# Three query chunks from the un-normalised residual, gates chunk by chunk, all centrings of one norm on VectorE

## The chip, the cores and the metric

The kernel runs on one core of a Trainium2 chip. The metric is the device time of one execution in microseconds (us), the median of three. The core has TensorE (PE in the rows, its weight loads PEld), VectorE (DVE), ScalarE (ACT), GpSimd (POOL) and SyncE (SP, which here only issues transfers).

## What is computed

A two-layer backbone on 512 latent tokens and 256 context tokens, D_MODEL = 1024, all in float32. Layer 0 mixes by latent attention and retention, layer 1 by a bidirectional mLSTM; a SwiGLU feed-forward (FFN) and layer norms follow each mixer. The change lies at the seam of the two layers, where the last norm of layer 0 feeds the input projection of layer 1:

```python
x = _layer_norm(ALPHA * x + ml[5] * _swiglu(_modulate(x, ml[3], ml[4]), ffn_w_in[l], ffn_w_out[l]),
                ln_g[l, 1], ln_b[l, 1])

def _mlstm_project(h, w_in, conv_w, conv_b, gate_b):
    qk, v, og, g = jnp.split(h @ w_in, [o1, o2, o3], axis=-1)
    qk = jax.nn.silu(_centred_conv(qk, conv_w, conv_b))
    q, k = jnp.split(qk, 2, axis=-1)
    ...
    g = (g.reshape(b, s, 4, H_M) + gate_b).astype(jnp.float32).transpose(2, 0, 3, 1)
    fwd = (g[0], jax.nn.log_sigmoid(g[1]))
    bwd = (g[2], jax.nn.log_sigmoid(g[3]))
```

Here `h` is the normalised and modulated `x`; `x` carries on as the residual.

## The kernel before

Tokens lie along the free axis: a 128x768 tile is 128 features of all 768 tokens, and `xT` holds eight of them (k or m = 0 to 7), so a norm over features is a sum over partitions, made by TensorE with a matrix of ones. Every float32 weight is split in two parts: ScalarE rounds it into a high part, GpSimd subtracts to get the low part, and a product is three matmuls (high x high, high x low, low x high), each in pieces of 512 and 256 columns. Weights come through a ring of four slots that SyncE fills. A slot's next load is issued when its last reader is done. Each engine runs its own list of instructions in the order written, and they meet only in counting semaphores, so one waiting instruction holds up all that is written behind it on its engine.

**The order at the seam.** The FFN of layer 0 ends with eight down-projection tiles (m = 0 to 7). VectorE merges each into `xT` (L2584), adds it to the running sum (L2595) and the square that ScalarE makes (L1872) to the other (L2609). TensorE then makes, from the un-normalised residual, two "query" feature chunks (f = 0, 1) of the mLSTM's input projection: `zqhi` and `zqlo` are the residual times the gain, split in two (L2150 on ScalarE, L2650 on VectorE), and the chunk is 24 matmuls for each f, as pieces of 258 and 256 columns over k (L1458). The mean and the deviation are put in afterwards, by `late_query` on VectorE (L2663 to L2667). `LN_AFTER = 3` puts the two sums of the norm (`ln_sums(1)`, L1340) after k = 2. Chunks f = 0 to 3 take weights that are loaded and split ahead (`fx_split` on ScalarE, L1911, `fx_low` on GpSimd, L3194); for f = 0 and 1 they go into slots of the FFN's weights that fall free with down tile 5 and down tile 7.

**The norm.** `layer_norm(1)` centres the tiles (x - mean), VectorE six (L2621) and GpSimd two (L3162), and VectorE multiplies each by 1/deviation (L2631). ScalarE makes the modulated `hT1[k]` (L1711, L1716) and VectorE its low part `hlo1[k]` (L2386), which counts `input_lo`.

**The projection.** `m_chunk(f, k)` is three matmuls for f < 4 (latent tokens alone) and six for f >= 4. Chunks 2 and 3 run together over k, chunk 3 `LAG` = 2 steps behind, and each step takes one unit of the modulation rows of layer 1 (L988: 16 matmuls of 256 columns, weights straight from the ring). The gates' projection, eight times six matmuls with `wg`, follows as one block, and then f = 4 to 7, each 48 matmuls, whose weight `whi1` and `wlo1` are a ring load, a split on ScalarE (L1695) and a subtraction on GpSimd (L3168). Chunks 0 to 7 are then convolved on VectorE (`conv(f)`, L2955 to L2957), from `cpad`, which ScalarE fills (`conv_in`: L2181 for f = 0, 1, and L2188, L2190 from the bank of PSUM for the others), and ScalarE's Silu follows (L2197, L2199). VectorE's list goes: late queries, modulation rows, conv(0), conv(1), `g_` (L2970, waits for the gates' evacuation L2209 on ScalarE), `lf` (L2974, waits for ScalarE's logarithm L2214), scans, conv(2), scans, conv(3), conv(4) to conv(7). TensorE's token-major tiles (L1024 to L1026) reuse the banks of chunks 5 to 7, and the third and later wait for their evacuation.

`LAG` is also read at the head of the kernel, where input chunks 0 and 1 of layer 0 run together over k in the same manner.

Of the kernel before, what the change touches and what calls it, by code (L numbers as in the profile page):

```python
# [126 lines left out]
def build(nc, x, c, ctx, c_ctx, mod_w, mod_b, ln_g, ln_b, ffn_w_in, ffn_w_out, ab_w_in, mla_q_norm, mla_w_uq,  # L127
# [354 lines left out]
    N_FX, N_Q, MOD_PRE = 4, 2, 3  # L482
    FX_ORDER, LN_AFTER = (2, 3, 0, 1), 3
# [179 lines left out]
    LAG = 2  # L663
# [162 lines left out]
    SUB_DVE, LEAD = KD - 2, 3  # L826
# [124 lines left out]
    def _(pe):  # L951
# [499 lines left out]
        for k in range(KD):
# [3 lines left out]
            for f in range(N_Q):  # L1455
                for w, z, st, sp_ in ((0, zqhi, k == 0, False), (0, zqlo, False, False), (1, zqhi, False, k == KD - 1)):
                    for a, b, at in Q_MM:
                        mm = pe.matmul(q_bank(f)[:, at:at + b - a], fx_chunk(f, w, k), z[:, k, a:b], start=st, stop=sp_)  # L1458
# [3 lines left out]

        rows2, rows3 = PS[2][:, T:], PS[3][:, T:]
        pe.wait_ge(ln_mean, 2)
        pe.wait_ge(ln_var, 2)
# [4 lines left out]
        mod_rows_stacked(1, 2, rows2, MOD_PRE, KD - 1)  # L1470
# [196 lines left out]
    def _(act):  # L1667
# [300 lines left out]
        def gate_loads():  # L1968

            act.dma_start(wgr[:, :, :], m_w_in[0].rearrange("(k p) n -> p k n", p=P)[:, :, C_MG:C_MG + 4 * H_M]).then_inc(gate_in, 16)  # L1970
            for g in range(4):
                act.dma_start(gb[32 * g:32 * g + H_M, :], m_gate_b[0, g].unsqueeze(1)).then_inc(gate_in, 16)

        def ffn(l):
# [75 lines left out]
            for at, (kind, i) in enumerate(seq):  # L2050
# [87 lines left out]
                else:  # L2138
# [1253 lines left out]
```

## Time and profile before

| | |
|---|---|
| median of 3 runs | 1805.11 us (1803.15 to 1807.51) |
| the profiled execution | 1806.19 us, its span 1804.5 us |
| PE busy | 1709.8 us (95 % of the span) |
| DVE, ACT, POOL busy | 998.3, 746.3, 855.4 us (55, 41, 47 %) |
| mean granted clock of TensorE | 0.985 of 2.4 GHz |

The rows below are of this one execution. Its own time is 1.69 us above its span and 1.08 us above the median. TensorE has work for 95 % of the span, so a time is gained or lost where TensorE stands idle, runs at the lower clock, or gets another amount of work. A row of a timeline has the start, the duration, engine and line, the operation, output and inputs with their shape, and, in brackets, how long the engine had stood idle before it and what released it.

### The profile page before, as it was taken

The page shows a single profiled execution, that of the slowest core. Times are in us where ns is not written, and L with a number is a line of the kernel's source. Part 1 is how long each engine was busy: PE and PEld are TensorE (multiplying, and loading weights), DVE is VectorE, ACT ScalarE, POOL GpSimd, SP SyncE. Part 2 cuts the span into 40 slices and gives each one's busy share as a digit, 9 for nine tenths or more (in the row PEclk, how much of TensorE's full clock was granted, in tenths as well). Part 3 has the DMA queues.
Part 4 walks back from the last instruction along what each step waited for, and adds up shares of the span by engine and source line. Part 5 has one row for each costly group of instructions (what it writes and reads, how often), then busy time and mean ns, then how long its engine had stood idle before and what let it go on. Part 6 is the DMA issues. An engine that isn't in the chain of part 4 may idle for free. (4 is left out here: it accounts for less than half of the span.)

```text
span 1804.5 us, 25317 instructions
## 1 busy us (share of the span) xinstructions
PE 1709.8 (95%) x10068; PEld 1436.5 (80%) x10068; DVE 998.3 (55%) x1622; ACT 746.3 (41%) x1151; POOL 855.4 (47%) x491
## 2 busy tenths in 40 slices
PE   4999999999899999999999997999978999999997
PEld 2888767755487889999999995877767879889886
DVE  2133345666567866464646679850287885333354
ACT  1531323655434853232323346452435583333344
POOL 1342212166536366464544651342335757566475
PEclk8999999999999999999999999999989999999999
DMA  9312242265412121212122243322201323333231
GB/s 349 89 47 59 59 140 94 94 185 172 135 47 71 47 70 59 82 56 84 49 78 63 71 132 127 101 59 70 59 1 47 94 70 118 94 94 115 72 117 59
DMA packets 189515, 163.81 MB, mean 91 GB/s; under 512 B 17742, under 2 KB 168494, under 8 KB 189398
## 3 DMA queue, kind: packets, MB, share of 16 engines
q1 hardware_dynamic: 187616, 160.92, 29.3%
q8 instruction: 80, 1.31, 0.3%
q10 hardware_dynamic: 1782, 1.28, 0.2%
q14 instruction: 37, 0.30, 0.1%
HBM read 160.08 MB, written 2.10 MB: 90 GB/s over the span
## 5 line engine op out<-in xcount | busy, mean ns | idle before, releaser
L3214 POOL TENSOR_TENSOR wsplit<-wsplit_raw,wsplit 128x512 fp32r<-128x512 f32 x108 | 149.8, 1407 | 118.4 <-DVE wsplit_raw L2753 105.6
L2584 DVE SCALAR_TENSOR_TENSOR xT<-ps,modc,xT 128x512 f32<-128x512 f32 (+1 forms) x168 | 104.1, 657 | 150.0 <-PE ps L1036 128.0
L1036 PE MATMUL ps<-us_a,wsplit 128*128 128x512 f32 x864 | 179.9, 355 | 3.1 <-DVE us_a L2854 1.7
L3199 POOL TENSOR_TENSOR wsplit<-ring,wsplit 128x1024 fp32r<-128x1024 f32 (+1 forms) x48 | 112.3, 2353 | 112.3 <-ACT wsplit L1918 112.3
L1036 PEld LDWEIGHTS ps<-us_a,wsplit 128*128 128x128 f32 x864 | 142.2, 188 | 27.8 <-DVE us_a L2854 2.4
L1036 PE MATMUL ps<-h,wsplit 128*128 128x512 f32 x720 | 156.0, 377 | 1.0 <-DVE hu L2677 1.0
L1930 ACT ACTIVATE wsplit<-wsplit_raw 128x512 fp32r<-128x512 f32 x108 | 68.4, 633 | 204.0 <-DVE wsplit_raw L2753 204.0
L1036 PE MATMUL ps<-us_b,wsplit 128*128 128x512 f32 x720 | 151.1, 354 | 1.7 <-DVE us_b L2854 1.7
L1036 PEld LDWEIGHTS ps<-h,wsplit 128*128 128x128 f32 x720 | 127.8, 188 | 26.1 <-DVE hu L2677 1.2
L3214 POOL TENSOR_TENSOR wsplit<-ring,wsplit 128x512 fp32r<-128x512 f32 x81 | 115.4, 1436 | 61.0 <-ACT wsplit L1930 61.0
L1036 PEld LDWEIGHTS ps<-us_b,wsplit 128*128 128x128 f32 x720 | 118.4, 188 | 21.5 <-DVE us_b L2854 2.1
L3168 POOL TENSOR_TENSOR wsp_in<-ring,wsp_in 128x1024 fp32r<-128x1024 f32 x22 | 53.1, 2413 | 163.1 <-ACT wsp_in L1695 163.1
L3289 POOL TENSOR_SCALAR lnbuf<-lnbuf,den 128x768 f32<-128x768 f32 (+1 forms) x48 | 84.9, 1775 | 88.5 <-DVE den L2542 87.9
L1026 PE MATMUL ps<-h,wsplit 128*128 128x384 f32 (+1 forms) x396 | 126.8, 320 | 0.0
L1025 PE MATMUL ps<-h,wsplit 128*128 128x384 f32 (+1 forms) x396 | 126.8, 320 | 0.0
L1024 PE MATMUL ps<-h,wsplit 128*128 128x384 f32 (+1 forms) x396 | 126.7, 320 | 0.0
L1036 PE MATMUL ps<-hx,wsp_in 128*128 128x512 f32 (+3 forms) x666 | 123.2, 346 | 2.5 <-DVE hx L2386 2.0
L3179 POOL TENSOR_TENSOR wsplit<-ring,wsplit 128x1024 fp32r<-128x1024 f32 x34 | 91.8, 2706 | 61.7 <-ACT wsplit L1938 61.7
L1036 PEld LDWEIGHTS ps<-hx,wsp_in 128*128 128x128 f32 (+1 forms) x666 | 102.8, 188 | 22.7 <-issue 3.7
L1024 PE MATMUL ps<-ts,wsplit 128*128 128x384 f32 (+1 forms) x360 | 112.9, 314 | 0.0
L1025 PE MATMUL ps<-ts,wsplit 128*128 128x384 f32 (+1 forms) x360 | 112.9, 314 | 0.0
L1026 PE MATMUL ps<-ts,wsplit 128*128 128x384 f32 (+1 forms) x360 | 112.9, 314 | 0.0
(495 smaller groups left out, 3959.8 us busy)
## 6 DMA issues: line engine op xcount, KB each, us to landing
ring<-in_ffn_w_in SPq DMA_DIRECT2D x88, 512.0 KB, 3.8
ring<-in_mod_w SPq DMA_DIRECT2D x77, 512.0 KB, 4.5
ring<-in_ffn_w_out SPq DMA_DIRECT2D x40, 512.0 KB, 3.4
ring<-in_m_w_in SPq DMA_DIRECT2D x24, 512.0 KB, 3.7
ring<-in_ab_w_in SPq DMA_DIRECT2D x21, 512.0 KB, 3.9
mod_rest<-in_mod_w SPq DMA_DIRECT2D x10, 512.0 KB, 15.8
ring<-in_ab_w_out SPq DMA_DIRECT2D x8, 512.0 KB, 4.3
ring<-in_m_w_out SPq DMA_DIRECT2D x8, 512.0 KB, 4.0
```

The costliest lines, as they stand in the source:

```text
L1024: pe.matmul(dst, s_hi, m_hi, start=first, stop=False)
L1025: pe.matmul(dst, s_hi, m_lo, start=False, stop=False)
L1026: return pe.matmul(dst, s_lo, m_hi, start=False, stop=last)
L1036: mm = pe.matmul(dst[:, a:b], w, h[:, a:b], start=st, stop=sp_)
L1930: act.activation(w_op(l, p, o, 0), src, ACT.Copy).then_inc(s_hi, 1)
L2584: ins = dve.scalar_tensor_tensor(xT[:, m, a:b], pair[:, a:b], modc[:, l, g, m, v:v + 1], xT[:, m, a:b], ALU.mult, ALU.add)
L3168: pool.tensor_tensor(w_lo[:, i % 2, :], ring[:, n % RING, :], w_hi[:, i % 2, :].bitcast(F32), ALU.subtract).then_inc(lo_made, 1)
L3179: pool.tensor_tensor(w_unit(place, 1), ring_unit(n), w_unit(place, 0).bitcast(F32), ALU.subtract).then_inc(lo_made, 1)
L3199: pool.tensor_tensor(down_unit(l, g, q, 1), down_ring(l, g, q), down_unit(l, g, q, 0).bitcast(F32), ALU.subtract).then_inc(lo_made, 1)
L3214: pool.tensor_tensor(w_op(l, p, o, 1), src, w_op(l, p, o, 0).bitcast(F32), ALU.subtract).then_inc(s_lo, 1)
L3289: pool.tensor_scalar(probs(i)[:, a:T], probs(i)[:, a:T], den[:, 1, i:i + 1], None, ALU.mult).then_inc(att_p, 1)
```

## The change

It touches eight things around the seam.

1. `N_Q` 2 to 3: query chunk 2 is made from the un-normalised residual too, after the sums of the norm (`q_part(2, k)`, 48 matmuls of 258 and 256 columns in place of 24 of 512), and takes a third `late_query`. The banks are dealt anew.
2. `LN_AFTER` 3 to 6: the sums of the norm come after k = 5.
3. VectorE makes all eight centrings of norm 1 (`SUBS`), GpSimd none.
4. The gates' projection runs chunk by chunk as `hlo1[k]` comes, with `m_chunk(3)` three steps behind (`LAG` 3, in the head too) and one unit of modulation rows behind each `m_chunk(3)`.
5. `late_query(0)` goes into VectorE's loop of the norm (at k = 2), and the low parts follow one step behind, not two.
6. The gates' weights are split before the norm, and their zeroing goes from GpSimd (one memset) to ScalarE (four of 128x512).
7. `fx_split` and `fx_low` for f = 0, 1 stand at m = 2 and 4, before at m = 3 and 5. On SyncE the loads of `mod_pre` stand behind the four loads of the fx weights, before ahead of them.
8. TensorE's waits ahead of f = 4 to 7 are placed anew.

```diff
-    N_FX, N_Q, MOD_PRE = 4, 2, 3
-    FX_ORDER, LN_AFTER = (2, 3, 0, 1), 3
+    N_FX, N_Q, MOD_PRE = 4, 3, 3
+    FX_ORDER, LN_AFTER = (2, 3, 0, 1), 6
...
-        return PS[(0, 1, 2, 3, 0, 2, 3, 0)[f]]
+        return PS[(0, 1, 2, 0, 2, 1, 3, 0)[f]]
...
-    LAG = 2
+    LAG = 3
...
-    SUB_DVE, LEAD = KD - 2, 3
+    SUBS, LEAD = (KD - 2, KD, KD - 2), 3
...
-        mod_rows_stacked(1, 2, rows2, MOD_PRE, KD - 1)
+        mod_rows_stacked(1, 2, rows2, MOD_PRE, KD - 3)
+        pe.wait_ge(ln_mean, 2)
+        for k in range(KD):
+            mm = q_part(2, k)
+            if k < 3:
+                mod_rows_stacked(1, 2, rows2, KD - 3 + k, KD - 2 + k)
+        mm.then_inc(ffn_tile, 1)
...
-        rest = [(1, 2, rows2, KD - 1)] + [(1, 3, rows3, k) for k in range(KD)]
+        pe.wait_ge(gate_lo, 1)
+        pe.wait_ge(ln_var, 2)
         for k in range(KD + LAG):
             if k < KD:
                 pe.wait_ge(input_lo, 2 * KD + k + 1)
-            for f, kf in ((2, k), (3, k - LAG)):
...
-            if k < len(rest):
-                l, g, rows, n = rest[k]
-                mod_rows_stacked(l, g, rows, n, n + 1)
-        pe.wait_ge(gate_lo, 1)
-        pe.wait_ge(late_q, 2)
-        for k in range(KD):
-            mm = project(PS[1], wg[:, 0, k, :], wg[:, 1, k, :], hT1[:, k, :], hlo1[:, k, :], k == 0, k == KD - 1, ALL_SEGS)
-        mm.then_inc(gate_mm, 1)
+                mm = project(PS[3], wg[:, 0, k, :], wg[:, 1, k, :], hT1[:, k, :], hlo1[:, k, :], k == 0, k == KD - 1, ALL_SEGS)
+                if k == KD - 1:
+                    mm.then_inc(gate_mm, 1)
+            if k >= LAG:
+                if k == LAG:
+                    pe.wait_ge(late_q, 1)
+                mm = m_chunk(3, k - LAG)
+                mod_rows_stacked(1, 3, rows3, k - LAG, k - LAG + 1)
+        mm.then_inc(ffn_tile, 1)
         mod_columns(1, 2, rows2)
         for f in range(4, 8):
+            if f == 4:
+                pe.wait_ge(late_q, 3)
...
             if f == 6:
+                pe.wait_ge(gate_ev, 4)
+            if f == 7:
                 pe.wait_ge(mod_ev, MOD_AT[1, 3])
-            if f >= 5:
-                pe.wait_ge(f_ev, f - 2)
+                pe.wait_ge(f_ev, 4)
...
-                        if l == 0 and m in (3, 5):
+                        if l == 0 and m in (2, 4):
                             fx_split(2 + m // 4)
...
-                layer_norm(1, lambda k: low_chunk(2, k, hT1, hlo1, hlo1_raw))
                 dve.wait_ge(gate_hi, 1)
...
-                for f in range(N_Q):
-                    late_query(f)
-                mod_rows_stacked(1, 2, PS[2][:, T:])
+                layer_norm(1, lambda k: low_chunk(2, k, hT1, hlo1, hlo1_raw), between=lambda k: late_query(0) if k == 2 else None, lag=1)
+                late_query(1)
+                late_query(2)
+                mod_rows_stacked(1, 2, PS[1][:, T:])
...
-                        pool.memset(wg[:, :, :, :].bitcast(F32), 0.0).then_inc(gate_zero, 1)
...
-            if l == 0:
-                pool.wait_ge(zq_lo, KD)
-                layer_norm(1)
```

**TensorE in the loop of the projection.** Before, in its last steps and at the start of the gates' block (`ps3<-hT1,fx1_hi` is chunk 3, `ps3<-ring,scol` a modulation unit; a unit's first matmul waits for its slot):

```order
L1036 MATMUL ps3<-hT1,fx1_lo 128x512
L988 MATMUL ps3<-ring,scol 2x256 [waits landed1]
L988 MATMUL ps3<-ring,scol 2x256 x3
...
L1036 MATMUL ps3<-hT1,fx1_hi 128x512
L1036 MATMUL ps3<-hlo1,fx1_hi 128x512
L1036 MATMUL ps3<-hT1,fx1_lo 128x512
L1036 MATMUL ps1<-hT1,wg 128x512 [waits late_q,gate_lo]
L1036 MATMUL ps1<-hT1,wg 128x256
```

After, in one step of the loop and at its end:

```order
L1040 MATMUL ps3<-hT1,wg 128x512 [waits input_lo]
L1040 MATMUL ps3<-hT1,wg 128x256
L1040 MATMUL ps3<-hlo1,wg 128x512
...
L1040 MATMUL ps3<-hT1,wg 128x256
L1040 MATMUL ps0<-hT1,fx1_hi 128x512
L1040 MATMUL ps0<-hlo1,fx1_hi 128x512
L1040 MATMUL ps0<-hT1,fx1_lo 128x512
L992 MATMUL ps0<-ring,scol 2x256 [waits landed3]
L992 MATMUL ps0<-ring,scol 2x256 x3
...
L992 MATMUL ps0<-ring,scol 2x256 [waits landed2]
L992 MATMUL ps0<-ring,scol 2x256 x3
L1002 MATMUL ps1<-kc,mrow 128x2 [waits mod_row]
L1002 MATMUL ps1<-kc,mrow 128x2 x7
L1040 MATMUL ps2<-hT1,whi1 128x512 [waits lo_made,late_q]
```

The gates' matmuls stand in the loop, a modulation unit comes only behind each chunk-3 step, so that three units follow the last gate matmuls, and the first matmul of chunk 4 (`whi1`) stands right behind the loop with the columns of modulation rows between.

**TensorE in the head**, where chunks 0 (`ps0`) and 1 (`ps1`) of layer 0's input run together. Before:

```order
L1036 MATMUL ps0<-hx,wsp_in0 128x512 [waits input_lo,lo_made]
...
L1036 MATMUL ps0<-hx,wsp_in0 128x256
L1036 MATMUL ps1<-hx,wsp_in0 128x512 [waits input_lo,lo_made]
L1036 MATMUL ps1<-hx,wsp_in0 128x256
```

After, from the same place:

```order
L1040 MATMUL ps0<-hx,wsp_in0 128x512 [waits input_lo,lo_made]
...
L1040 MATMUL ps0<-hx,wsp_in0 128x256
L1040 MATMUL ps0<-hx,wsp_in0 128x512 [waits input_lo,lo_made]
...
L1040 MATMUL ps0<-hx,wsp_in0 128x256
L1040 MATMUL ps1<-hx,wsp_in0 128x512 [waits input_lo,lo_made]
L1040 MATMUL ps1<-hx,wsp_in0 128x256
```

One more step of chunk 0 stands ahead of the first of chunk 1, and one more of chunk 1 is left for the end.

**ScalarE during the last down tiles** (`sg<-xT` the square of a tile, `zqhi` the gain times it, `wsplit<-ring` the split of a query weight). Before:

```order
L1872 ACTIVATE sg<-xT 128x768 [waits ln_sum2,z_ev]
L2150 ACTIVATE zqhi<-xT,gain 128x512
L1872 ACTIVATE sg<-xT 128x768 [waits ln_sum2,z_ev]
L2150 ACTIVATE zqhi<-xT,gain 128x512
L1911 ACTIVATE wsplit<-ring 128x2x512 [waits ffn_tile,landed0]
...
L1872 ACTIVATE sg<-xT 128x768 [waits ln_sum2,z_ev]
L2150 ACTIVATE zqhi<-xT,gain 128x512
L1911 ACTIVATE wsplit<-ring 128x2x512 [waits ffn_tile,landed1]
L1872 ACTIVATE sg<-xT 128x768 [waits ln_sum2,z_ev]
```

After:

```order
L1881 ACTIVATE sg<-xT 128x768 [waits ln_sum2,z_ev]
L2171 ACTIVATE zqhi<-xT,gain 128x512
L1920 ACTIVATE wsplit<-ring 128x2x512 [waits ffn_tile,landed0]
L1881 ACTIVATE sg<-xT 128x768 [waits ln_sum2,z_ev]
L2171 ACTIVATE zqhi<-xT,gain 128x512
L1881 ACTIVATE sg<-xT 128x768 [waits ln_sum2,z_ev]
...
L2171 ACTIVATE zqhi<-xT,gain 128x512
L1920 ACTIVATE wsplit<-ring 128x2x512 [waits ffn_tile,landed1]
L1881 ACTIVATE sg<-xT 128x768 [waits ln_sum2,z_ev]
```

The split that waits for down tile 5 stood ahead of the square of tile 3 and stands ahead of that of tile 2; the other, which waits for tile 7, moved from tile 5 to tile 4.

## Rows read from the trace of the kernel before

**Rows 1.** TensorE's waits, 1040 to 1200 us: waiter, releaser, total us, times, longest

```profile
PE ps L1458 <- POOL wsplit L3194: 3.8, 1, 3.8
PE ps L1024 <- ACT cpad L2190: 2.2, 1, 2.2
PE ps L1340 <- DVE lnbuf L2595: 2.0, 1, 2.0
PE ps L1036 <- DVE hlo L2386: 1.9, 1, 1.9
PE ps L1036 <- issue: 0.9, 1, 0.9
```

**Rows 2.** Stretches: start:end length, busy of PE, PEld, DVE, ACT, POOL, granted clock

```profile
1090.20:1096.30 6.10, 6.06 (x36) 5.87 (x36) 6.00 (x9) 1.46 (x2) 0.00 (x0) 0.72 0.28 86
...
1177.50:1184.00 6.50, 4.17 (x17) 2.77 (x16) 6.43 (x5) 4.51 (x9) 5.51 (x5) 1.00 0.29 82
```

**Rows 3.** ScalarE's timeline from 1141 us: start, duration, operation, idle before

```profile
1141.58 0.89 ACT L2209 ACTIVATE li<-ps,again 8x768 f32<-8x768 f32 x1 [4.93 <-PE ps L1036]
...
1144.33 0.90 ACT L2209 ACTIVATE gt<-ps,again 8x768 f32<-8x768 f32 x1
...
1182.31 0.60 ACT L2188 ACTIVATE cpad<-ps 128x512 f32<-128x512 f32 x1 [1.05 <-DVE cacc L2957]
```

**Rows 4.** VectorE's timeline, the gates' chain and one convolution that nothing held

```profile
1139.75 2.80 DVE L2957 SCALAR_TENSOR_TENSOR cacc<-cpad,vcol,cacc 128x512 f32<-128x512 f32 x1
1145.26 1.75 DVE L2970 SCALAR_TENSOR_TENSOR gbc<-gt 8x1536 f32<-8x1536 f32 x1 [2.71 <-ACT gt L2209]
...
1151.45 1.75 DVE L2974 SCALAR_TENSOR_TENSOR lf<-gt,lf 8x1536 f32<-8x1536 f32 x1 [2.55 <-ACT lf L2214]
...
1171.16 0.75 DVE L2957 SCALAR_TENSOR_TENSOR cacc<-cpad,vcol,cacc 128x512 f32<-128x512 f32 x1
```

**Rows 5.** VectorE's timeline in the norm, and of a late query

```profile
1108.19 0.95 DVE L2631 TENSOR_TENSOR xT<-xT,lnbuf 128x768 f32<-128x768 f32 x1
1109.06 0.94 DVE L2621 TENSOR_TENSOR xT<-xT,lnbuf 128x768 f32<-128x768 f32 x1
...
1127.38 0.16 DVE L2663 COPY again<-ps 128x2 f32<-128x2 f32 x1
...
1129.09 0.15 DVE L2663 COPY again<-ps 128x2 f32<-128x2 f32 x1
```

**Rows 6.** TensorE's timeline in the projection's loop and at its end

```profile
1123.72 0.61 PE L988 MATMUL ps<-ring,scol 128*2 128x256 f32 x8
...
1125.86 0.61 PE L988 MATMUL ps<-ring,scol 128*2 128x256 f32 x8
...
1132.89 0.52 PE L1036 MATMUL ps<-hT,wg 128*128 128x512 f32 x2
...
1141.41 0.65 PE L998 MATMUL ps<-kc,mrow 2*128 2x2 f32 x8
1141.99 0.62 PE L1036 MATMUL ps<-hT,whi 128*128 128x512 f32 x2
```

**Rows 7.** SyncE's next issue into the ring

```profile
1126.53 0.38 SPq L834 DMA_DIRECT2D ring<-in_m_w_in  x1
```

**Rows 8.** Transfers from 1124 to 1142 us: count, size, median us to landing

```profile
ring<-in_m_w_in SPq DMA_DIRECT2D x5, 512.0 KB, 4.3
```

**Rows 9.** GpSimd's timeline from 1135 us

```profile
1135.16 2.57 POOL L3168 TENSOR_TENSOR wlo<-ring,whi 128x1024 fp32r<-128x1024 f32 x1 [1.78 <-ACT whi L1695]
1137.73 1.44 POOL L3154 TENSOR_SCALAR xT<-xT,again 128x512 f32<-128x512 f32 x1
1139.14 2.85 POOL L3168 TENSOR_TENSOR wlo<-ring,whi 128x1024 fp32r<-128x1024 f32 x1
```

**Rows 10.** The head: GpSimd's subtraction and TensorE's wait for it

```profile
61.63 2.38 POOL L3168 TENSOR_TENSOR wsp_in<-ring,wsp_in 128x1024 fp32r<-128x1024 f32 x1 [16.44 <-ACT wsp_in L1695]
...
64.07 0.50 PE L1036 MATMUL ps<-hx,wsp_in 128*128 128x512 f32 x1 [0.57 <-POOL wsp_in L3168]
```

More of the change, by code:

```diff
@@ L921, in _ @@
             unit(n, view(n % RING, KD), w_in[:, :, f * P:(f + 1) * P])
+        sp.wait_ge(prod, BASE[1][0]["prod"])
+        for k in range(MOD_PRE):
+            sp.dma_start(mod_pre[:, k, :], mod_w[1, k * P:(k + 1) * P, 2 * D:3 * D]).then_inc(mod_pre_in, 16)
         mod_units(1, 2, MOD_PRE)
@@ L1447, in _, with q_part @@
         ffn(0)
+        def q_part(f, k):
+            for w, z, st, sp_ in ((0, zqhi, k == 0, False), (0, zqlo, False, False), (1, zqhi, False, k == KD - 1)):
+                for a, b, at in Q_MM:
+                    mm = pe.matmul(q_bank(f)[:, at:at + b - a], fx_chunk(f, w, k), z[:, k, a:b], start=st, stop=sp_)
+            return mm
         pe.wait_ge(zq_cols, 1)
@@ L1454, in _ @@
             pe.wait_ge(zq_lo, k + 1)
[L1455 to L1458 removed]
+            for f in range(2):
+                mm = q_part(f, k)
                 if k == KD - 1:
                     mm.then_inc(ffn_tile, 1)
[L1463 to L1465 removed]
+        rows2, rows3 = PS[1][:, T:], PS[0][:, T:]
         pe.wait_ge(mod_pre_in, 16 * MOD_PRE)
@@ L1972, in gate_loads, with gate_weights @@
                 act.dma_start(gb[32 * g:32 * g + H_M, :], m_gate_b[0, g].unsqueeze(1)).then_inc(gate_in, 16)
+            for part in range(2):
+                for k in (0, KH):
+                    ins = act.activation(wg[:, part, k:k + KH, :], kc[:, 0:KH * P].rearrange("p (k n) -> p k n", k=KH), ACT.Copy, scale=0.0)
+            ins.then_inc(gate_zero, 1)
+        def gate_weights():
+            act.wait_ge(gate_in, 16 * 5)
+            act.wait_ge(gate_zero, 1)
+            for g in range(4):
+                ins = act.activation(wg[:, 0, :, 32 * g:32 * g + H_M], wgr[:, :, H_M * g:H_M * (g + 1)], ACT.Copy)
+            ins.then_inc(gate_hi, 1)
         def ffn(l):
@@ L2158, in ffn @@
             if l == 0:
+                gate_weights()
                 layer_norm(1)
@@ L2168, in _ @@
         from_norm(1, hT1, hlo1_raw)
-        act.wait_ge(gate_in, 16 * 5)
-        act.wait_ge(gate_zero, 1)
-        for g in range(4):
-            ins = act.activation(wg[:, 0, :, 32 * g:32 * g + H_M], wgr[:, :, H_M * g:H_M * (g + 1)], ACT.Copy)
-        ins.then_inc(gate_hi, 1)
         def conv_in(f):
@@ L2200, in conv_out @@
                 act.activation(mk[:, f - 4, LAT:T], cacc[:, f % 2, LAT + 2:T + 2], ACT.Silu, bias=bias).then_inc(silu_ev, 1)
-        for f in range(N_Q):
+        for f in range(2):
             conv_in(f)
@@ L2609, in square_sum, with layer_norm @@
                 dve.tensor_tensor(s2_[:, 0:nt], s2_[:, 0:nt], sq_[:, m % 2, 0:nt], ALU.add).then_inc(ln_sum2, 1)
-        def layer_norm(i, split, between=None):
+        def layer_norm(i, split, between=None, lag=2):
             nt = NT[i // 2]
@@ L3160, in layer_norm @@
             pool.wait_ge(ln_mean, i + 1)
-            for k in range(SUB_DVE, KD):
+            for k in range(SUBS[i], KD):
                 pool.tensor_tensor(xT[:, k, 0:nt], xT[:, k, 0:nt], lnm[:, 0:nt], ALU.subtract).then_inc(ln_subp, 1)
```

67 lines of the change are left out of this document (32 added, 35 removed).

## The prediction

> **What bounds the kernel now.** I read the profile in this order: the table of TensorE's waits around the seam, to see how much idle time there is to win; then, backwards from the last of those waits, the timelines of ScalarE, VectorE and TensorE, to see which chain sets its end. From 1040 to 1200 us TensorE waits five times for 0.9 to 3.8 us [rows 1], and after the first it runs a while at half clock (0.72 of full over 1090.2 to 1096.3, [rows 2]). At first sight these 10.8 us are what the change is after. But the second largest, 2.2 us for ScalarE's `cpad` L2190, ends last: token tiles start again at 1183.2 only when chunk 7 has left its bank. That evacuation starts at 1182.3, released by VectorE's convolution L2957 [rows 3], and VectorE is busy for 6.43 of the 6.50 us around it, TensorE for 4.17 [rows 2]. So **VectorE's list, not TensorE's work, decides when TensorE goes on at 1183.2.** Whatever TensorE saves ahead of that only lengthens this wait, and it could come 2.2 us later at no cost. Followed back, VectorE's list stood idle last at 1151.4, for ScalarE's `lf`, and before that at 1145.3, for the last evacuation of the gates, L2209 [rows 4]. Those four evacuations start at 1141.6, with the end of the gates' block of matmuls [rows 3]. The chain is: gates done, 4 x 0.92 us on ScalarE, `g_` at 1145.26, logarithm, `lf` at 1151.45, then scans and convolutions to 1182.2. The question is when `g_` starts in the changed kernel.
>
> **The parts.**
>
> *Query chunk 2, `LN_AFTER`, the moved splits.* 48 matmuls of 258 and 256 columns stand in for 24 of 512: the same columns, a few per cent more. The wait of 3.8 us for the weights of the query chunks is gated by down tile 7, ScalarE's split and GpSimd's low part, all of which stay; the split moved to m = 2 makes ScalarE wait there for tile 5, so the squares come no earlier, and I leave 1090.2 where it is. The sums behind k = 5 take away the 2.0 us wait, and the loop to k = 7 ends some 3 us earlier. It moves the norm itself by +0.8 us (from 1102.2 to about 1103.0, since three more steps of 1.43 us stand ahead of the sums). All this is ahead of the wait at 1183.2 and counts only through the norm.
>
> *The norm.* VectorE makes two centrings more, 0.87 us each by the pitch of rows 5, and one late query in the loop, 1.71 us (the distance of the two copies in [rows 5]). The two centrings of GpSimd beside VectorE's first three are gone, so that the deviation, not the centrings, comes last, which pays for the later start: tile 0 is multiplied at about 1107.9 (before 1108.19). Then by the new list five operations to the first low part, 1107.9 + 5 x 0.87 = 1112.3; three more to each next, 1114.9; with the late query 1119.2; 1121.9.
>
> *The loop of the gates.* A step was 2.14 us (two chunks and a unit, from 1123.72 to 1125.86 [rows 6]). A gate piece is 1.06 us (eight from 1132.89 to 1141.41 [rows 6]), a chunk piece 0.70 (three matmuls of 0.23). The new step is 2.14 - 0.70 + 1.06 = 2.50 us. TensorE waits about 0.9 and 1.5 us for low parts 2 and 3 and is ahead of VectorE no more from step 3, at 1121.9. The last gate piece ends at 1121.9 + 4 x 2.5 + 1.06 = 1133.0, 8.4 us sooner than before. If ScalarE could evacuate at once, `g_` would follow at 1136.7. It can't: in ScalarE's list the splits of chunk 4's and chunk 5's weights stand ahead of the gates' evacuation, and these now come late.
>
> *The ring.* The weights of chunk 4 take the slot of modulation unit 4 of the second group. Before, this unit ended at 1126.47 [rows 6] and the load was issued at 1126.53 [rows 7]. Now a unit comes only behind each chunk-3 step: unit 0 in step 3, unit 4 in step 7, which ends at 1121.9 + 5 x 2.5 - 0.2 = 1134.2, and units 5 to 7 at 1.43 us each. So the load for chunk 4 goes out at **1134.2 instead of 1126.5, 7.7 us later**. It lands 4.3 us (median [rows 8]) to 4.9 us later, at 1138.5 to 1139.1; that for chunk 5, issued at 1135.7, lands at about 1140.0 to 1140.6. ScalarE (about 1 us a split, 0.7 a `cpad`) splits the first to 1140.0, fills `cpad` of chunk 1, splits the second to about 1141.3, and only then evacuates the gates: 4 x 0.92 = 3.7, to 1145.0 against 1145.23 before [rows 3]. **The 8.4 us that the gates gain are given back whole to this order of ScalarE's list.**
>
> *Convolution 1.* It needs that `cpad`, ready at 1140.7, and stands ahead of `g_`. GpSimd's subtraction for chunk 4 starts at 1140.1, and for chunk 5 at about 1143.4, 2.57 and 2.85 us long with 1.44 between [rows 9]. Before, the last step of this convolution took 2.80 us from 1139.75 and ended with GpSimd's subtraction, begun at 1139.14 [rows 4, 9], where an undisturbed one takes 0.75 [rows 4]: each of the two waits out the other. The Trainium skill ("SBUF — State Buffer", Who interferes with whom) says that an operation of VectorE with two inputs in SBUF and one of GpSimd that reads it shut each other out for the whole instruction; the trace agrees at this convolution. By that rule taking the centrings from GpSimd pays in the norm, and costs nothing here. I let its three steps alternate with GpSimd's: it starts at 1142.5, and ends at about 1147.4. Bounds: unhindered it would end by 1142.7 and the evacuation decides (`g_` at 1145.0, that is -0.25 us); held for one more GpSimd operation it ends at 1149. I take 1147.4 as nearest to the two holds of rows 4 and 9. `g_` moves from 1145.26 to 1147.45, **+2.2 us**.
>
> *Behind it.* Chunk 4 needs its low part, 1142.4: TensorE, through with loop and columns at 1139.2, waits 3.3 us, a new wait, and goes on at 1142.5 against 1141.99. If a stretch at half clock follows, as after the wait of 3.8 us (a loss of 6.1 x 0.28 = 1.7 us [rows 2]), it reaches the token tiles 2.2 us later than before, less the 0.9 us wait that goes: still ahead of VectorE's end at 1182.2 + 2.2. So the wait at 1183.2 moves by VectorE's +2.2.
>
> *The head.* Chunk 0 ends one step sooner: TensorE was continuous, a step is 1.05 us, but it waits 0.3 us for a low part on the way, so 0.7 to 0.8 us sooner. ScalarE's split and GpSimd's subtraction (from 61.63) come forward, and the wait of 0.57 us [rows 10] goes; 0.3 us of it is paid for by the new wait. **-0.3 us**; between 0 and -0.57.
>
> *Hidden at nothing:* the zeroing on ScalarE (it waits for tiles there), the memset off GpSimd, the order of SyncE's loads, the new banks, the third late query (VectorE waits for `cpad` 1 anyway).
>
> **Sum.** +2.2 - 0.3 = +1.9 us. The profiled execution, 1806.19 us, would be 1808.1; the median of before is 1.08 lower, and 1805.11 + 1.9 gives **1807.0 us**.
>
> **The rivals.** (a) *The evacuation decides, not convolution 1.* It falls between GpSimd's operations: -0.25 - 0.3, **1804.5**. For it: the convolution's start and GpSimd's are within 0.7 us, and the order is open. (b) *Fewer collisions behind `g_`.* VectorE and GpSimd meet again some four times before 1182; a shift can undo one or two, each worth 2.80 - 0.75 = 2.05 us. With conv(1) free as well VectorE would be 0.25 + 4.1 earlier; but TensorE, 0.5 later at chunk 4 and 0.9 earlier by the wait that goes, then sets the end, at 2.2 + 0.4 = 2.6 us sooner: 1805.1 - 0.3 - 2.6 = **1802.2**. Against it: the three engines shift by about the same 2 us, so that the pattern stays. (c) *The other side: a longer hold of VectorE's chain.* One more collision, +2.05, or the weights of chunk 5 land a microsecond late because TensorE's short waits at steps 2 and 3 bring the half clock (1.7 us [rows 2], which delays unit 4 and all behind it by as much): 1807.0 + 1.7 to 2.05 = 1808.7 to 1809.1, with both **1810.8**, with one about 1809. It decides once `g_` starts after 1149.2. (d) *The waits that the change takes from TensorE reach the end* (2.0, 1.9 and 0.9 us [rows 1]): 1805.1 - 4.8 = **1800.3**. This holds only if the wait at 1183.2 isn't the chain that I read it as, and if chunk 4's weights come before the loop ends.
>
> **Chances.** Forecast 0.45, (a) 0.2, (b) 0.06, (c) 0.22, (d) 0.07. A measurement of this kernel can tell 0.2 %, 3.6 us, from no change: faster is under 1801.5, slower above 1808.7. (d) and a little of (b) are faster, 0.09; (c) is slower, and 0.06 of the forecast's case by its upper bound for convolution 1 (1149), together 0.28; the rest, 0.63, lies between. The range, 1802.0 to 1810.5, leaves out (d) and the upper part of (c), about half of it.
>
> **What would show it.** After, in the profile: TensorE's wait before chunk 4 (`whi`), 3 us, released by GpSimd's subtraction (L3168 before); the first `in_m_w_in` load issued near 1134; ScalarE's gate evacuations ending at 1145.0 with idle ahead of the splits for the transfer; VectorE's `g_` near 1147.4 with no idle before it; the token tiles' wait ended near 1185.4. The prediction is wrong if `g_` starts before 1144, if the wait for `cpad` is gone, or if TensorE's clock falls in the loop of the gates.

## The result: slower, by more than the range allowed

Both kernels were run ten times.

| | before | after |
|---|---|---|
| median of 10 runs | 1806.29 us (1803.15 to 1815.83) | 1815.35 us (1812.25 to 1820.33) |
| the profiled execution, its span | 1806.19, 1804.5 us | 1812.25, 1810.3 us |
| PE busy | 1709.8 us | 1714.0 us |
| mean granted clock of TensorE | 0.985 | 0.985 |

The ratio is 1.0040, 95 % interval 1.0026 to 1.0055: the changed kernel is 4.7 to 9.9 us slower. The forecast was 1.9 us slower, with a range that ended at 1810.5.

**How the two traces are laid over each other.** The two profiled executions differ by 1.4 us before the seam, in the transfers at the start, so from here on times at the seam are counted from the first query matmul (1090.22 us in the trace before, 1088.79 after). The middle column has what the forecast gives on the same count:

| us from the first query matmul | before | forecast | after |
|---|---|---|---|
| the last query matmul ends | 19.1 | | 26.4 |
| first low part `hlo1[0]` starts | 23.2 | 22.1 | 27.4 |
| gates' last matmul ends | 51.3 | 42.8 | 50.8 |
| load for chunk 4 issued | 36.3 | 44.0 | 52.1 |
| gates' evacuation ends | 55.0 | 54.8 | 62.6 |
| chunk 4 starts | 51.8 | 52.3 | 59.7 |
| `g_` starts | 55.0 | 57.2 | 63.7 |
| token tiles go on | 93.0 | 95.2 | 101.7 |

`g_` is 8.67 us later than before and the token tiles go on 8.67 us later: the chain that the forecast followed is the one that decides, and it is 6.5 us later still than forecast. Behind it 1.4 us come back: from that point to the end it is 621.3 us before and 619.8 after. One stretch there, 1300 to 1400 us, had a mean granted clock of 0.88 before and 0.95 after. Nothing shows that this comes from the change: among the changed kernel and the experiments built on it, this last part runs from 619.8 to 623.3 us, and the first query matmul comes between 1088.7 and 1093.8, though the edits all lie between the two.

The table of TensorE's waits from 1040 to 1200 us after, which answers to [rows 1] (waiter, releaser, total us, times, longest):

```profile
PE ps L1040 <- DVE hlo L2405: 5.8, 4, 2.1
PE ps L1455 <- POOL wsplit L3216: 4.0, 1, 4.0
PE ps L1040 <- POOL wlo L3190: 2.7, 1, 2.7
PE ps L1028 <- ACT cpad L2209: 1.9, 1, 1.9
```

Of the waits that the change was to take away, the 2.0 us for the sums and the 0.9 us are gone. The wait of 2.7 us before chunk 4 came as forecast (3.3). But the 1.9 us for low parts have grown to 5.8, where the forecast had 0.9 and 1.5. VectorE and ScalarE, from 1090 to 1160 us, show who is behind it:

```profile
DVE hlo L2405 <- ACT hT L1725: 7.8, 4, 5.9
...
ACT hT L1725 <- PE ps L1455: 6.3, 1, 6.3
```

The high part `hT1[0]` waits for a query matmul. ScalarE's timeline, VectorE's, and TensorE's, each from the after trace:

```profile
1107.76 1.31 ACT L1720 ACTIVATE hlo_raw<-xT,gain 128x512 f32<-128x512 f32 x2 [1.09 <-DVE xT L2650]
1115.34 0.84 ACT L1725 ACTIVATE hT<-hlo_raw 128x768 fp32r<-128x768 f32 x1 [6.27 <-PE ps L1455]
```

```profile
1106.70 0.96 DVE L2650 TENSOR_TENSOR xT<-xT,lnbuf 128x768 f32<-128x768 f32 x1 [0.46 <-ACT lnbuf L1892]
...
1116.21 0.96 DVE L2405 TENSOR_TENSOR hlo<-hlo_raw,hT 128x768 fp32r<-128x768 f32 x1 [5.94 <-ACT hT L1725]
1117.09 0.95 DVE L2650 TENSOR_TENSOR xT<-xT,lnbuf 128x768 f32<-128x768 f32 x1
```

```profile
1117.32 0.58 PE L1040 MATMUL ps<-hT,wg 128*128 128x512 f32 x2 [2.08 <-DVE hlo L2405]
...
1119.83 0.89 PE L1040 MATMUL ps<-hT,wg 128*128 128x512 f32 x2 [1.22 <-DVE hlo L2405]
...
1124.14 1.01 PE L1040 MATMUL ps<-hT,wg 128*128 128x512 f32 x2 [2.14 <-DVE hlo L2405]
...
1126.74 1.01 PE L1040 MATMUL ps<-hT,wg 128*128 128x512 f32 x2 [0.31 <-DVE hlo L2405]
```

Up to the first multiplication (1106.70, that is 17.9 on the common count; forecast 17.7, before 18.0) all is as forecast. Then ScalarE has `hlo1_raw[0]` ready and stands until TensorE has ended query chunk 2. The cause is a line that the diff doesn't touch:

```python
if i == 2 and k == 0:
    act.wait_ge(ffn_tile, q_made(N_Q - 1))
```

`hT1` lies in memory over `zqhi` and half of `zqlo`, the operands of the query chunks, and may be written only when their last reader is done. With `N_Q` = 2 this waits for chunk 1, which ended at 19.1; with `N_Q` = 3 it waits for chunk 2, which ends at 26.4. And because VectorE's list has the first low part ahead of the third multiplication (`lag=1`), VectorE stands for the same time, with six multiplications still to do. TensorE then waits for low parts four times, and from 1116 to 1131 us its mean granted clock is 0.66 (windows: start:end, length, busy of PE, PEld, DVE, ACT and POOL, clock), and behind the wait for chunk 4 it is 0.50:

```profile
1116.00:1131.00 15.00, 10.01 (x36) 6.76 (x37) 14.21 (x19) 11.91 (x18) 0.00 (x0) 0.66 0.00 1
1148.44:1154.00 5.56, 5.56 (x17) 4.78 (x18) 5.49 (x4) 2.88 (x4) 5.56 (x3) 0.50 0.90 215
```

The rest of the chain is the forecast's, shifted. Load, split, evacuation and `g_` after, on SyncE, ScalarE and VectorE, answering to [rows 7, 3, 4]:

```profile
1140.89 0.38 SPq L838 DMA_DIRECT2D ring<-in_m_w_in  x1
```

```profile
1144.75 1.06 ACT L1704 ACTIVATE whi<-ring 128x1024 fp32r<-128x1024 f32 x1 [10.22 <-DMA ring<-in_m_w_in]
...
1146.80 1.06 ACT L1704 ACTIVATE whi<-ring 128x1024 fp32r<-128x1024 f32 x1 [0.38 <-DMA ring<-in_m_w_in]
...
1150.50 0.90 ACT L2228 ACTIVATE gt<-ps,again 8x768 f32<-8x768 f32 x1
```

```profile
1146.46 2.12 DVE L2977 TENSOR_SCALAR cacc<-cpad,vcol 128x512 f32<-128x512 f32 x1 [4.55 <-ACT cpad L2200]
1148.61 1.14 DVE L2978 SCALAR_TENSOR_TENSOR cacc<-cpad,vcol,cacc 128x512 f32<-128x512 f32 x1
1149.79 2.79 DVE L2979 SCALAR_TENSOR_TENSOR cacc<-cpad,vcol,cacc 128x512 f32<-128x512 f32 x1
1152.50 1.74 DVE L2992 SCALAR_TENSOR_TENSOR gbc<-gt 8x1536 f32<-8x1536 f32 x1
```

The gates' last matmul has long ended (1139.6) when ScalarE comes to evacuate it at 1147.8, and `g_` has no idle time ahead of it, since convolution 1, held by GpSimd, ends later than the evacuation: both as the forecast has them.

### The profile page after: what moved, and what is told of

It is laid out like the page before. It is cut to its first block and busy times, and to the rows that moved or that the text cites. A ratio compares the mean times of both kernels' runs of the same rounds, so it can differ in the third digit from the quotient of the medians.

```text
span 1810.3 us, 25370 instructions
## 1 busy us (share of the span) xinstructions
PE 1714.0 (95%) x10092; PEld 1439.4 (80%) x10092; DVE 994.3 (55%) x1628; ACT 748.5 (41%) x1155; POOL 849.0 (47%) x488
## 3 DMA queue, kind: packets, MB, share of 16 engines
q10 hardware_dynamic: 1782, 1.28, 0.2%
## 5 line engine op out<-in xcount | busy, mean ns | idle before, releaser
L1040 PEld LDWEIGHTS ps<-us_a,wsplit 128*128 128x128 f32 x864 | 142.2, 188 | 27.4 <-DVE us_a L2874 2.4
L1040 PEld LDWEIGHTS ps<-us_b,wsplit 128*128 128x128 f32 x720 | 118.4, 188 | 21.5 <-DVE us_b L2874 2.1
```

Source lines behind the costliest of these rows:

```text
L1040: mm = pe.matmul(dst[:, a:b], w, h[:, a:b], start=st, stop=sp_)
```

## The experiments

Eleven kernels were run. Their ratios are against the kernel before, on the same chip and in the same rounds (e4, run once, has no ratio and stands in its own part). On the common count:

| kernel | low part 0 | last low part | gates end | chunk 4 load | `g_` | tiles go on | ratio (95 %) |
|---|---|---|---|---|---|---|---|
| before | 23.2 | 35.7 | 51.3 | 36.3 | 55.0 | 93.0 | 1 |
| after | 27.4 | 45.2 | 50.8 | 52.1 | 63.7 | 101.7 | 1.0040 (1.0026 to 1.0055) |
| e1 | 22.6 | 40.3 | 44.4 | 45.7 | 57.2 | 95.2 | 1.0014 (1.0000 to 1.0029) |
| e2 | 27.4 | 45.1 | 52.8 | 48.1 | 60.4 | 98.4 | 1.0030 (1.0015 to 1.0046) |
| e3 | 22.6 | 40.3 | 46.1 | 41.6 | 54.5 | 92.5 | 0.9998 (0.9983 to 1.0014) |
| e5 | 21.4 | 39.2 | 44.6 | 45.9 | 58.6 | 96.5 | 1.0019 (1.0006 to 1.0033) |
| e6 | 22.6 | 40.3 | 46.1 | 41.6 | 54.6 | 92.6 | 1.0006 (0.9993 to 1.0020) |
| e7 | 22.6 | 40.3 | 46.1 | 41.6 | 50.5 | 90.7 | 0.9988 (0.9977 to 1.0000) |
| e8 | 27.4 | 41.9 | 46.0 | 47.3 | 59.0 | 96.9 | 1.0016 (1.0003 to 1.0028) |
| e9 | 23.2 | 39.9 | 46.1 | 41.6 | 50.6 | 90.5 | 0.9979 (0.9964 to 0.9994) |
| e10 | 21.5 | 39.2 | 45.1 | 40.5 | 49.7 | 89.7 | 0.9976 (0.9962 to 0.9989) |
| e11 | 23.3 | 39.9 | 44.9 | 40.1 | 50.2 | 90.2 | 0.9980 (0.9967 to 0.9994) |

The times follow the column "tiles go on": by the middle of its interval each kernel differs from the one before by what the tiles differ in its trace, within 1.5 us (after: 7.2 us by the time, 8.7 by the tiles; e2: 5.4 and 5.4; e5: 3.4 and 3.5; e10: -4.3 and -3.3). Intervals of neighbouring kernels overlap, so single steps of 1 to 4 us rest on the dates in the traces, not on the times.

### e1: query chunk 2 ahead of the modulation products

```diff
+        pe.wait_ge(ln_mean, 2)
+        for k in range(KD):
+            mm = q_part(2, k)
+        mm.then_inc(ffn_tile, 1)
         for k in range(MOD_PRE):
...
-        mod_rows_stacked(1, 2, rows2, MOD_PRE, KD - 3)
...
+        mod_rows_stacked(1, 2, rows2, MOD_PRE, KD)
...
+            if f == 1:
+                dve.wait_ge(unit_done, UB["mod12"] + KD)
```

> The changed kernel with one order on TensorE altered: the eight pieces of query chunk 2 stand right behind query chunks 0 and 1, ahead of the modulation products; VectorE's second late query waits for those products. Theory A (ScalarE may write the first high part hT only when query chunk 2 is done, 6.3 us of idle there in the changed kernel, and everything behind it is late by that): chunk 2 ends about 1109 instead of 1115.2, the wait before ScalarE's L1725 falls from 6.3 us to about 0.3, the first low part comes at 1111 instead of 1117.2, g_ on VectorE starts about 6 us sooner (near 1146.5 instead of 1152.5) and the time falls by 6 to 8 us, to that of the kernel before within 2 us. Rival B (the late ring loads decide, whatever the norm does): they follow the loop, so they come as much sooner; B can't be told from A by this run alone, only by the size: if g_ moves by less than 3 us, A is wrong. Rival C (the half clock in the loop of the gates, 13 us of it, is the loss, and it comes from having chunk pieces wait on low parts at all): the clock is again 0.5 over 10 us or more, and the time falls by less than 4 us.

Measured: the wait before the first high part is 1.38 us (expected was 0.3), and the first low part follows at once (ScalarE, then VectorE of e1):

```profile
1115.53 0.84 ACT L1723 ACTIVATE hT<-hlo_raw 128x768 fp32r<-128x768 f32 x1 [1.38 <-PE ps L1455]
```

```profile
1116.40 0.96 DVE L2403 TENSOR_TENSOR hlo<-hlo_raw,hT 128x768 fp32r<-128x768 f32 x1 [1.06 <-ACT hT L1723]
```

`g_` comes 6.5 us sooner than in the changed kernel, at 57.23, and the kernel is 1.0014 of the one before, 2.5 us by the middle of the interval. By the middles the time fell by 4.7 us, less than the 6 to 8 expected. Theory A holds. Rival C, by which the half clock would stay and most of the loss with it, falls: TensorE has no stop for a low part, and the clock is 0.66 over 5 us behind its wait for the ring and 1.00 over the 10 us after. What is left, 2.2 us at `g_` and 2.2 us at the token tiles, has the size of the forecast's own term for ring, ScalarE's order and convolution 1.

### e2: modulation units two a step

```diff
-                mod_rows_stacked(1, 3, rows3, k - LAG, k - LAG + 1)
+                if k - LAG < 4:
+                    mod_rows_stacked(1, 3, rows3, 2 * (k - LAG), 2 * (k - LAG) + 2)
...
         dve.wait_ge(gate_ev, 4)
+        dve.wait_ge(ffn_tile, q_made(3))
```

> The changed kernel with two modulation units behind each of the first four chunk-3 pieces, none behind the last four; VectorE's g_ also waits for the end of chunk 3. Query chunk 2 stays where it is. Theory A (the late start of the norm's output decides): ScalarE's 6.3 us wait and the low parts stay as they are; the load for chunk 4 is issued about 4 us sooner (1136.8 instead of 1140.9), the wait before chunk 4 (2.7 us) goes, and the gates' evacuation begins at 1143.8 instead of 1147.8, so g_ starts near 1148 and the time falls by 4 to 5 us; the rest, 2 to 4 us above the kernel before, stays. Rival B (the ring alone makes the loss): the time falls by all 6 to 9 us. Rival D (VectorE's chain behind g_ isn't what sets TensorE's end): g_ moves and the time doesn't, within 2 us.

The load for chunk 4 is issued 4.05 us sooner, as expected, and `g_` comes 3.3 us sooner, not 4.5: the loop itself, with more units in its first steps, ends later, and convolution 1 still alternates with GpSimd. The time fell by 1.8 us by the middles, where 4 to 5 were expected, and the intervals overlap (1.0030 against 1.0040). The shift of 3.3 us at the token tiles stands in the trace alone. Rival B (the ring alone) falls: most of the loss is still there. Rival D falls too, by the traces: in every kernel up to e6 the tiles go on 38 us behind `g_` (37.9 to 38.0).

### e3: both

The edits of e1 and e2 together.

> Both edits of the two runs before. If the two causes add, g_ starts near 1142 in the trace's time, 10 us sooner than in the changed kernel, and TensorE's wait before the token tiles is gone, so that TensorE's own work sets the end: 3 to 5 us below the kernel before. If one of them hides the other, the time is that of the better of the two.

The causes add nearly in full: `g_` at 54.5, the tiles at 92.5, the time that of the kernel before (0.9983 to 1.0014). The 10 us at `g_` were 9.2, but TensorE's wait before the token tiles stays (1.94 us): VectorE's chain still sets the end, because convolution 1 ends at 54.5 though the gates' evacuation ends at 52.2. The 3 to 5 us below the kernel before didn't come; that part of the expectation was wrong.

### e4: the head alone

```diff
-                for k in range(KD + LAG):
+                for k in range(KD + 3):
...
-                    if k >= LAG:
-                        feature_chunk(1, (k - LAG,))
+                    if k >= 3:
+                        feature_chunk(1, (k - 3,))
```

> The kernel before with the lag of the head alone set to 3. Forecast's term: 0.3 us less, seen in the trace as TensorE's wait of 0.57 us for wsp_in gone and a new stop of 0.3 us inside the first 18 pieces; nothing else moves.

It was run once: 1805.15 us. TensorE in the head of e4:

```profile
44.97 3.79 PE L1036 MATMUL ps<-hx,wsp_in 128*128 128x512 f32 x12 [2.29 <-DVE hx L2386]
48.92 18.25 PE L1036 MATMUL ps<-hx,wsp_in 128*128 128x512 f32 x102 [0.16 <-DVE hx L2386]
```

The wait for `wsp_in` [rows 10] is gone and a stop of 0.16 us has come. But counted from the matmul with which this stretch starts (46.16 before, 44.97 here) the same matmul 30 us further on comes after 30.39 us before, 30.40 in e4 and 30.37 in the changed kernel. The term is 0.0, not -0.3.

### e5: the wait piece by piece

```diff
+            if k < KD - 1:
+                mm.then_inc(mod_act, 1)
...
-                if i == 2 and k == 0:
+                if i == 2 and k < 4:
+                    act.wait_ge(mod_act, 2 + (2, 3, 5, 6)[k])
+                if i == 2 and k == 4:
                     act.wait_ge(ffn_tile, q_made(N_Q - 1))
...
+            if f == 1:
+                dve.wait_ge(unit_done, UB["mod12"] + KD)
```

> The changed kernel with nothing reordered: ScalarE's single wait for the end of query chunk 2, ahead of the first high part hT, becomes a wait for the piece of chunk 2 that last reads the bytes which each hT overwrites (pieces 1, 2, 4, 5 and 7 for hT 0 to 4). Counted from the first query matmul: Theory A (the coarse wait makes the norm's output late): the 6.3 us stop before L1725 goes, the first low part starts at 22.3 (27.4 in the changed kernel), g_ at 57.2 (63.7), as it did with chunk 2 moved (22.6 and 57.2), and the time falls by 5 to 7 us. Rival E (the move of chunk 2 helped because the modulation units left the stretch ahead of it, not by the wait): g_ stays above 61.

Nothing is reordered here, and the stop of 6.27 us becomes 0.25:

```profile
1110.86 0.84 ACT L1729 ACTIVATE hT<-hlo_raw 128x768 fp32r<-128x768 f32 x1 [0.25 <-PE ps L1455]
```

The first low part starts at 21.4 and `g_` at 58.6, 5.1 us sooner than in the changed kernel; rival E falls. By the middles the time fell by 3.8 us, where 5 to 7 were expected. `g_` is 1.3 us later than in e1, which was not expected: the weights of chunk 4 are split at 50.8 here and at 49.5 in e1, with the load issued 0.2 us apart, so this transfer took 1.1 us longer. The wait is thereby shown as the cause by two different edits, one that moves what is waited for and one that makes the wait finer. What they have in common besides is a wait of VectorE's second late query, which stands behind all low parts and has no idle time ahead of it in e1 (it starts at 1135.03, as the last low part ends).

### e6 and e7: ScalarE's order, then VectorE's

e6 is e3 with:

```diff
-        for f in range(2):
-            conv_in(f)
-            split_high("in1", f + N_FX, whi1)
+        conv_in(0)
+        conv_in(1)
+        split_high("in1", N_FX, whi1)
...
                            bias=gb[32 * g:32 * g + H_M, :]).then_inc(gate_ev, 1)
+        split_high("in1", N_FX + 1, whi1)
```

> The kernel with both edits (query chunk 2 first, two modulation units a step), and in ScalarE's list both cpad of chunks 0 and 1, then the split for chunk 4, the gates' evacuation, and only then the split for chunk 5. Theory F (ScalarE's list holds the gates back): the evacuation ends at 50.5 after the first query matmul (52.2 in the kernel with both edits). g_ still stands behind convolution 1 and comes at 52.5 to 54.5 (54.5). Time 0 to 2 us less than with both edits. Rival: the split for chunk 5, 4 us later, makes TensorE wait before chunk 5 instead, and nothing is won.

e7 has in addition:

```diff
         conv(0)
-        conv(1)
         dve.wait_ge(gate_ev, 4)
...
         dve.scalar_tensor_tensor(g_, z_, -1.0, z_, ALU.mult, ALU.min).then_inc(row_dve, 1)
+        conv(1)
```

> The same, and VectorE makes convolution 1 behind g_ instead of ahead of it. Theory: g_ follows the evacuation at 50.6, lf at 56.8 (61.2 in the kernel before), VectorE's chain no longer sets the end, TensorE's wait before the token tiles falls under 0.5 us, and they go on at 90.2 (93.0 in the kernel before): 2 to 3.5 us faster than the kernel before. Rival G (the collisions with GpSimd that convolution 1 leaves return behind g_): lf comes at 56.8 and the token tiles still go on after 92.

e6: the evacuation ends 1.6 us sooner (50.5 against 52.2), and nothing comes of it, `g_` at 54.6: convolution 1 stands ahead of it. e7: `g_` follows the evacuation at 50.5. VectorE of e7:

```profile
1140.42 2.08 DVE L2994 SCALAR_TENSOR_TENSOR gbc<-gt 8x1536 f32<-8x1536 f32 x1 [0.16 <-ACT gt L2227]
1142.43 0.47 DVE L2979 TENSOR_SCALAR cacc<-cpad,vcol 128x512 f32<-128x512 f32 x1
1142.94 2.82 DVE L2980 SCALAR_TENSOR_TENSOR cacc<-cpad,vcol,cacc 128x512 f32<-128x512 f32 x1
1145.79 1.15 DVE L2981 SCALAR_TENSOR_TENSOR cacc<-cpad,vcol,cacc 128x512 f32<-128x512 f32 x1
...
1148.76 1.74 DVE L2999 SCALAR_TENSOR_TENSOR lf<-gt,lf 8x1536 f32<-8x1536 f32 x1
```

The collision is there still (2.82 us for a step of 0.75), and `lf` has no idle time ahead of it, at 58.8, not 56.8; before it had 2.55 us of idle [rows 4]. So 4.1 us at `g_` became 2.0 at `lf` and 1.8 at the token tiles (90.7 against 92.6 of e6). Rival G is right for about half of it. TensorE's wait before the token tiles, which was expected to fall under 0.5 us, is still 1.9. The kernel is 2 us below the one before by the middle of an interval that ends at no difference, 0.9977 to 1.0000.

### e8: low parts three steps behind

```diff
-between=lambda k: late_query(0) if k == 2 else None, lag=1)
+between=lambda k: late_query(0) if k == 2 else None, lag=3)
```

(on the changed kernel)

> The changed kernel with VectorE's low parts three steps behind the multiplications (one step in the changed kernel); ScalarE's wait for query chunk 2 stays. Theory H (the wait is made worse because the first low part stands in VectorE's list ahead of multiplication 2, so that VectorE stops 5.9 us too): the first low part stays at 27.4 after the first query matmul, but the later ones come at ScalarE's pace, 2.07 us, the last at 42 instead of 45.2; g_ 2 to 3 us sooner, near 61. Rival: the loop of the gates, at half clock, sets the pace, and g_ stays at 63.7.

ScalarE's wait stays and the first low part stays at 27.4, yet `g_` comes at 59.0, 4.75 us sooner, more than expected. VectorE works through the stop, and the low parts follow at ScalarE's pace. TensorE's first two stops in the loop are those of the changed kernel, 2.08 and 1.22 us, but the third and fourth don't come, and the granted clock over the same 15 us of the common count is 0.89, not 0.66:

```profile
1117.86:1132.86 15.00, 12.52 (x69) 8.45 (x69) 11.20 (x13) 14.78 (x23) 0.00 (x0) 0.89 0.20 58
```

`g_` is then 1.7 us behind e1's 57.2; with the changed kernel's order it is 6.5 behind. That 1.7 us is an estimate of what the wait costs with this list, since no kernel has the longer lag without the wait.

### e9: GpSimd's two centrings back

On e7, `SUBS` is (6, 6, 6) and GpSimd's `layer_norm(1)` is back.

> The kernel with all four edits (chunk 2 first, two units a step, ScalarE's and VectorE's order), and GpSimd makes centrings 6 and 7 of the norm again. Forecast's term: VectorE's first three centrings are held up by GpSimd (4.3 us instead of 2.7), the first multiplication comes 1.1 us later (deviation and centrings together), the two centrings saved later in VectorE's loop give 1.7 us back from multiplication 3 on: low part 7 within 0.7 us of where it was, time the same within 1.5 us. Rival: all centrings on VectorE are worth 1 to 2 us.

VectorE's three first centrings in e9:

```profile
1106.96 4.33 DVE L2640 TENSOR_TENSOR xT<-xT,lnbuf 128x768 f32<-128x768 f32 x3
1111.22 0.95 DVE L2650 TENSOR_TENSOR xT<-xT,lnbuf 128x768 f32<-128x768 f32 x1
```

GpSimd's two beside them:

```profile
1104.77 3.97 POOL L3187 TENSOR_TENSOR xT<-xT,lnbuf 128x768 f32<-128x768 f32 x2 [13.73 <-ACT lnbuf L1888]
```

The three take 4.33 us against 2.69 without GpSimd beside them. The first multiplication comes 1.8 us later than in e7 (expected was 1.1), and the first low part 0.7 us later, since in e7 VectorE had 1.06 us of idle ahead of it; but the last low part 0.4 us sooner, and the tiles 0.2 us sooner. 0.9979 against e7's 0.9988 lies within the intervals: no gain of having all centrings on VectorE is seen here, and the rival's 1 to 2 us falls. The rule that the prediction cited from the Trainium skill ("SBUF — State Buffer", Who interferes with whom) is borne out by the 4.33 us. That it pays in the norm to take the centrings from GpSimd is true of the first low part alone: the end of the loop depends on how much VectorE has to do in all, and there the two extra centrings take the gain back.

### e10: the piecewise wait with e7's orders, and e11

e10 is the changed kernel with the edits of e5, e2, e6 and e7; query chunk 2 and the first modulation units stay where the change put them.

> ScalarE's wait piece by piece (as in e5) with query chunk 2 and the modulation units in the changed kernel's order, two units a step in the loop, and ScalarE's and VectorE's order of e7. TensorE's stop of 3.2 us for the ring, which e7 has among its five units in a row, goes; stops of 0.8 and 1.3 us before gate pieces 2 and 3 come. Gates end within 0.5 us of e7's 46.1, token tiles at 90 to 91 after the first query matmul; time as e7's within 1.5 us.

TensorE's waits in e10:

```profile
PE ps L1455 <- POOL wsplit L3225: 4.0, 1, 4.0
PE ps L1028 <- ACT cpad L2214: 2.2, 1, 2.2
PE ps L1040 <- DVE hlo L2411: 2.1, 2, 1.3
PE ps L1002 <- DVE mrow L2386: 0.4, 1, 0.4
PE ps L1040 <- POOL wlo L3199: 0.3, 1, 0.3
```

It has the lowest ratio, 0.9976 (0.9962 to 0.9989), 4.3 us below the kernel before by the middle, with the tiles going on at 89.7 (93.0); e7, e9 and e11 lie within its interval or overlap it. The wait of 3.2 us for the ring is gone and that before chunk 4 nearly; the granted clock behind it is 1.00 (0.50 in the changed kernel):

```profile
1137.40:1143.00 5.60, 5.53 (x31) 4.89 (x32) 5.12 (x4) 4.77 (x5) 4.67 (x3) 1.00 0.53 151
```

e11 is e10 with GpSimd's two centrings and the first late query at k = 4.

> The kernel e10 with centrings 6 and 7 on GpSimd again (as in e9) and the first late query two steps later in VectorE's loop of the norm (at k = 4). Low part 3 needs 3.4 us less of VectorE's time ahead of it and starts 1 us later, so TensorE's stops before gate pieces 2 and 3 (0.8 and 1.3 us) shrink to less than 1 us together; the gates end at about 44 after the first query matmul (45.1), the token tiles follow 0.5 to 1 us sooner: 0 to 1.5 us less than e10. Rival: chunk 3's first piece now waits for the late query and takes the time back.

The two stops before gate pieces fell to one of 1.02 us, but a stop of 0.39 us came for the late query, and the stop for a modulation row later grew from 0.4 to 0.98 us. The tiles go on 0.5 us later than in e10, not sooner, and the time is the same, 0.9980 (0.9967 to 0.9994). The rival is right in part: the late query takes back some of what was won, the modulation row the rest.

## Why the prediction was wrong

**The step that failed is "five operations to the first low part"** in the part on the norm. It counts VectorE's operations from the new list, and takes for granted that ScalarE's high part is ready in between. I read there what VectorE has to do and not what ScalarE waits for; the waiting line is unchanged text, but it contains `N_Q`. The low part came at 27.4 and not 22.1, and all the dates behind it, the loop, the ring, the split, the evacuation, moved with it. The proof is e1, in which this wait is nearly gone: there `g_` starts at 57.23, where the forecast has 57.2, and the tiles go on 2.2 us later than before, where it has 2.2. That these agree so closely is luck in part. In e1 the gates end 1.6 us and the load goes out 1.7 us later than forecast, and the evacuation ends 1.5 us later; but the weights were ready for the split 3.8 us after the issue, not 4.3 to 4.9, and convolution 1 ended 6.0 us after its `cpad` was ready, not 6.7.

**A second step fell with it: the pace of the loop.** Against e1, the low parts are 4.8 us late from the first to the last, but the gates end 6.4 us late, and `g_` comes 6.5 us late. The 1.6 us between arise in the loop of the gates: four stops (0.9 and 1.5 us were forecast for two of them) with 0.66 of the clock over 15 us. The half clock was rival (c)'s mechanism, put at 1.7 us and in the same place, and the prediction had named a fall of the clock in this loop as a sign that it is wrong. In e8, with the first two stops alone, the clock is 0.89.

**What held.** VectorE's list, not TensorE, sets the time at which the token tiles go on (37.9 to 38.0 us behind `g_` in nine traces, those of before, after, e1 to e6 and e8). The ring: load, issue and split stand behind modulation unit 4, and ScalarE's list, with the splits ahead of the gates, gives the gates' gain back; e6 and e7 take that away. Convolution 1 is late by GpSimd. The new wait before chunk 4: 2.7 us, forecast 3.3. The waits that TensorE lost were worth nothing at the end. The first multiplication behind the centrings came at 17.9, forecast 17.7.

**What was off in size.** The head: 0.0 instead of -0.3 (e4). Behind the seam I took the rest as unmoved; this part is 1.4 us shorter than before in the changed kernel and up to 2 us longer in the experiments.

The chances were given to rivals of one chain. None of them asked whether another wait of the old kernel changes its meaning; the range of 8.5 us was made from the terms that I had, and so it left the result out.

**Left open.** How the 1.6 us of the loop divide between the lower clock and the stops themselves: no kernel has the one without the other. And why the chunk 4 transfer took 1.1 us longer in e5 than in e1.

## What to carry to other kernels

When a constant changes, look up every wait that is computed from it, also on lines that the diff doesn't show, and ask of each what memory it guards; here a tile that lies over another made one wait cost 6.5 us, more than any single order that was tuned. Where one engine's list puts the consumer of a late value ahead of its other work, the wait stops that engine too; a larger lag alone (e8) brought 4.75 of the 8.67 us at `g_` back. And a gain ahead of an in-order list comes out only if every entry between it and the chain is early as well: in e1 the gates were done 6.9 us sooner than before and `g_` came 2.2 us later. It took the earlier units (e2) and two reorderings (e6, e7) to bring `g_` 4.6 us ahead of the kernel before, of which 2.3 reached the token tiles.

## What the runs showed of the hardware

Five modulation units in a row, each a load of 512 KB into one of four slots, made TensorE wait 3.1 to 3.2 us for the ring in e1, e3, e6, e7 and e9. Behind it, in e1, a unit took 1.03 us in place of 0.61, at a granted clock of 0.66 over 5 us; with the same units spread between the query pieces (after, e10) this wait was 0.2 us or none. And two kernels that begin alike ended at different clocks: stops of 2.08 and 1.22 us before the first two later gate pieces stand in both the changed kernel and e8, with 0.66 and 0.89 of the clock over the 15 us in which they fall; the changed kernel has two stops more (2.14 and 0.31 us). Nor do equal stops give an equal clock: e5 stops for 0.84 and 1.28 us, e10 for 0.82 and 1.28, and over the same 15 us the clock was 0.89 in e5 and 1.00 in e10, which has more modulation units in these steps.
